# Inverse roots of queries, keys and attention results computed by GpSimd instead of VectorE

## The reference, cut to what matters

```python
h = rms_norm(x, ln_attn_g[i])
dq, dk, dv, mq, mk, mv = jnp.split(h @ w_in[i], cuts, axis=-1)   # six sections of 512 columns
dq = rms_norm(dq.reshape(B, S, 4, 2, 64), qk_norm_g[i, 0])       # likewise dk, mq, mk
y_diff = diff_attention(...)                                     # a = p0 - lam * p1, then
out = rms_norm(out, sub_g) * (1.0 - lam_init)                    # over 128 values of a head
x = x + jnp.concatenate([y_diff, y_moba], axis=-1) @ w_out[i]
x = x + conv_ffn(rms_norm(x, ln_ffn_g[i]), ...)
```

## Time and profile before

| | |
|---|---|
| median of three runs | 2059.21 us (2058.15 to 2059.31) |
| the profiled execution's own time | 2058.32 us |
| its span | 2056.1 us |
| mean granted TensorE clock | 0.997 of full |
| busy: PE, DVE, ACT, POOL | 2009.4, 1338.4, 957.1, 160.8 us |
| PE idle while the profile names a releaser or issue, longest group | 5.0 us in 6 times |
| layer 0 of the first block up to its feed forward | about the first 130 us |
| the same stage of layer 1 | about 350 to 465 us |

### The profile page before, as it was taken

One profiled execution on the slowest core, in us unless ns is written; L12 is line 12 of the kernel. 1 busy time (PEld: TensorE's weight loads), 2 busy tenths in 40 slices (PEclk: granted clock), 3 DMA queues, 4 the chain that ended last, 5 costly groups with the idle time before them and its releaser, 6 DMA issues.

```text
span 2056.1 us, 33524 instructions
## 1 busy us (share of the span) xinstructions
PE 2009.4 (98%) x13138; PEld 1738.2 (85%) x13138; DVE 1338.4 (65%) x2363; ACT 957.1 (47%) x1574; POOL 160.8 (8%) x169
## 2 busy tenths in 40 slices
PE   9999999999999999999999999999999999999998
PEld 7778998878999887878888788888878899888997
DVE  6767667767877348384445556868566595775675
ACT  4655555555555443353322453233246544455443
POOL 2001000000110100001200001111110000100110
PEclk9999999999999999999999999999999999999999
DMA  9447665535555422222222104534234244441654
GB/s 252 147 138 250 229 215 204 175 103 175 185 185 185 143 94 73 72 77 68 92 92 92 52 32 156 201 106 162 92 126 163 84 144 124 149 159 53 202 167 133
DMA packets 79707, 285.55 MB, mean 139 GB/s; under 512 B 8976, under 2 KB 9644, under 8 KB 79552
## 3 DMA queue, kind: packets, MB, share of 16 engines
q1 hardware_dynamic: 71136, 256.93, 37.6%
q10 hardware_dynamic: 6416, 19.51, 2.7%
q0 software_dynamic: 2000, 6.97, 1.3%
HBM read 277.55 MB, written 5.83 MB: 138 GB/s over the span
## 4 chain that ended last, share of the span: by engine, by line
PE 76%; DVE 13%; ACT 7%; issue 3%; DMA 1%; DVEq 0%; ACTq 0%; POOL 0%; SPq 0%
PE pb L1125 14%; PE pb L1127 14%; PE pb L1126 14%; PE pb L1138 6%; PE pb L1140 6%; PE pb L1139 6%; DVE SPL L2223 4%; ACT SPH L1638 3%; PE pb L1144 2%; PE pb L1303 2%; PE pb L1497 2%; PE pb L1304 2%; PE pb L1305 2%; PE pb L1478 2%; DVE GW L2556 1%
## 5 line engine op out<-in xcount | busy, mean ns | idle before, releaser
L2223 DVE TENSOR_TENSOR SPL<-RAW,SPH 128x1024 fp32r<-128x1024 f32 x460 | 559.4, 1232 | 387.0 <-ACT SPH L1638 366.1
L1638 ACT ACTIVATE SPH<-RAW 128x1024 fp32r<-128x1024 f32 x462 | 477.6, 1052 | 221.3 <-PE pb L1127 110.7
L1125 PE MATMUL pb<-HTH,SPH 128*128 128x256 f32 (+1 forms) x1304 | 445.7, 342 | 8.7 <-POOL HTL L2890 3.7
L1127 PE MATMUL pb<-HTH,SPL 128*128 128x256 f32 (+1 forms) x1304 | 436.6, 335 | 0.0
L1126 PE MATMUL pb<-HTL,SPH 128*128 128x256 f32 (+1 forms) x1304 | 436.2, 335 | 0.0
L1125 PEld LDWEIGHTS pb<-HTH,SPH 128*128 128x128 f32 x1304 | 246.6, 189 | 37.1 <-ACT HTH L1687 3.2
L1127 PEld LDWEIGHTS pb<-HTH,SPL 128*128 128x128 f32 x1304 | 246.7, 189 | 26.2
L1126 PEld LDWEIGHTS pb<-HTL,SPH 128*128 128x128 f32 x1304 | 246.5, 189 | 24.7
L1138 PE MATMUL pb<-SPH,HTH 128*128 128x512 f32 x640 | 254.4, 397 | 2.2 <-DVE SPL L2223 1.4
L1140 PE MATMUL pb<-SPL,HTH 128*128 128x512 f32 x640 | 249.9, 391 | 0.0
L1139 PE MATMUL pb<-SPH,HTL 128*128 128x512 f32 x640 | 249.7, 390 | 0.0
(11 more groups left out here) (298 smaller groups left out, 2869.4 us busy)
## 6 DMA issues: line engine op xcount, KB each, us to landing
RAW<-in_w_up SPq DMA_DIRECT2D x88, 512.0 KB, 4.6
RAW<-in_wa SPq DMA_DIRECT2D x64, 512.0 KB, 3.5
RAW<-in_w_in SPq DMA_DIRECT2D x48, 512.0 KB, 4.9
RAW<-in_wmg SPq DMA_DIRECT2D x48, 512.0 KB, 3.5
RAW<-in_wbr SPq DMA_DIRECT2D x48, 512.0 KB, 3.5
RAW<-in_w_down SPq DMA_DIRECT2D x44, 512.0 KB, 4.7
RAW<-in_w_ada SPq DMA_DIRECT2D x24, 512.0 KB, 4.8
ARAW<-in_w_ada ACTq DMA_DIRECT2D x24, 512.0 KB, 3.9
```

The costliest lines, as they stand in the source:

```text
L1125: T.matmul(o, wh[:, kt, :], xh[:, kt, n0:n1], start=kt == 0, stop=False)
L1127: m = T.matmul(o, wl[:, kt, :], xh[:, kt, n0:n1], start=False, stop=kt == 7)
L1638: A.activation(hi, raw, ACT.Copy, scale=1.0).then_inc(*act.tick(s["hi"], ("u", u)))
L2223: W.tensor_tensor(lo, raw, hi.bitcast(F32), SUB).then_inc(*dve.tick(s["lo_dve"], ("u", u)))
```

## The change

For layers 0 and 1 of the first block the roots are made on POOL. `qk_scale` gets a POOL part: two scalings with the mean's epsilon (16 values a partition in all), then one `pow` with a constant tile of -0.5. `y` gets a POOL part of four operations that depend on each other: multiply, scale and add, `pow`, multiply. They signal a new semaphore, `root_pool`. DVE keeps the sums and the multiplications into QKN and YN, and waits for `root_pool` where it computed roots before. The epsilon column SE loses its factors of c, since c belonged to the Newton steps. The new one-column tile HALF is filled at the start. POOL's `qk_scale` begins with waits on the memset of HALF, on `pool.last`, on DVE's sums and on SE.

```diff
--- before.py
+++ after.py
@@ -991,7 +991,7 @@
            "out_act",
            "lo_dve", "const_dve", "norm_dve", "qkv_dve", "soft_dve", "ffn_dve", "gla_dve", "branch_dve", "attn_dve",
            "out_dve",
-           "lo_pool", "norm_pool", "ffn_pool", "gla_pool", "branch_pool")
+           "lo_pool", "norm_pool", "ffn_pool", "gla_pool", "branch_pool", "root_pool")
 DMAS = ("raw0", "raw1", "raw2", "raw3", "raw4", "ada0", "ada1", "ada2", "x_in0", "x_in1", "par", "par2", "strips", "lamr", "const", "ctx", "bias",
         "table", "spill0", "spill1", "wdec", "x_back", "out")
 
@@ -2288,9 +2288,7 @@
         dve.wait_ge(n, ("sq", tag))
         rsqrt(n, ("rs", tag), sb["SS"][:, 4 + t0:6 + t0], sb["SS"][:, t0:t0 + 2], 1.0 / 1024, 2)
         if tag[0] == "a":
-            c = 0.375
-            W.tensor_scalar(sb["SE"][:, 0:2], sb["SS"][:, t0:t0 + 2], EPS / (1024 * c ** 2), (EPS / c) ** 2, MUL,
-                            ADD).then_inc(*dve.tick(n, ("se", tag)))
+            W.tensor_scalar(sb["SE"][:, 0:2], sb["SS"][:, t0:t0 + 2], EPS / 1024, EPS ** 2, MUL, ADD).then_inc(*dve.tick(n, ("se", tag)))
             return
         if tag[0] == "f":
             return
@@ -2345,12 +2343,8 @@
                             axis=AX.X, op=ADD, negate=None).then_inc(*dve.tick(q, ("qs", l, sec, t)))
 
     def qk_scale(l, sec):
-        q, QS = s["qkv_dve"], sb["QS"]
-        dve.wait_ge(q, ("qs", l, sec, 1))
-        dve.wait_ge(s["norm_dve"], ("se", f"a{l}"))
-        rsqrt(q, ("qr", l, sec), QS[:, 1, 0:16], QS[:, 0, 0:16], 1.0 / 64, 16,
-              [sb["SE"][:, t:t + 1] for t in range(2)])
-        dve.wait_ge(q, ("qr", l, sec))
+        QS = sb["QS"]
+        dve.wait_ge(s["root_pool"], ("qr", l, sec))
         for t in range(2):
             name = ("qkv", l, sec, t)
             if sec in (0, 1):
@@ -2416,16 +2410,7 @@
         dve.wait_ge(s["soft_act"], ("yq", l, g))
         W.tensor_reduce(out=sb["QSY"][:, 0, 0:4], in_=sb["SQY"][:, :].rearrange("p (g d) -> p g d", d=128), axis=AX.X,
                         op=ADD, negate=None).then_inc(*dve.tick(v, ("ys", l, g)))
-        dve.wait_ge(v, ("ys", l, g))
-        dve.wait_ge(v, ("r2", l, 4 * g + 3))
-        ss, rs = (sb["QSY"][:, i, 0:4].rearrange("p (i t) -> p i t", t=2) for i in range(2))
-        sums, squares = (V(R[:, i, 8 * g:8 * g + 1], [4, 2], [1, 2]) for i in (2, 3))
-        W.tensor_tensor(ss, ss, squares, MUL).then_inc(*dve.tick(v))
-        dve.wait_ge(*dve.last)
-        rsqrt(v, ("yr", l, g), sb["QSY"][:, 1, 0:4], sb["QSY"][:, 0, 0:4], 1.0 / 128, 4)
-        dve.wait_ge(v, ("yr", l, g))
-        W.tensor_tensor(rs, rs, sums, MUL).then_inc(*dve.tick(v))
-        dve.wait_ge(*dve.last)
+        dve.wait_ge(s["root_pool"], ("yr", l, g))
         W.tensor_tensor(yo, o, V(sb["QSY"][:, 1, 0:1], [2, per], [1, 2], [0, dv]), MUL).then_inc(
             *dve.free(*k.read(name)))
 
@@ -2830,6 +2815,7 @@
         for o, i in ((sb["OH"][0:32, 0:384], "onehot"), (sb["RB"][0:32, 0:12], "rel_bias"),
                      (sb["MROW"][0:12, 0:384], "maskrow")):
             G.dma_start(o, k.args[i]).then_inc(*pool.tick(s["strips"]))
+        G.memset(sb["HALF"][:, :], -0.5).then_inc(*pool.tick(s["root_pool"], "half"))
         G.memset(sb["QP1"][0:64, :, :], 0.0).then_inc(*pool.tick(s["gla_pool"]))
         pool.wait_ge(s["raw2"], ("u", 2))
         G.dma_start(sb["LAMR"][:, :], k.args["lamr"]).then_inc(*pool.tick(s["lamr"]))
@@ -2846,6 +2832,37 @@
         G.memset(sb["QP0"][64:128, base:base + 2, :], 0.0).then_inc(
             *pool.tick(s["gla_pool"], ("qp", l, sec, half)))
 
+    def qk_scale(l, sec):
+        QS, x = sb["QS"], sb["RS"][:, 0, 16:32]
+        pool.wait_ge(s["root_pool"], "half")
+        pool.wait_ge(*pool.last)
+        pool.wait_ge(s["qkv_dve"], ("qs", l, sec, 1))
+        pool.wait_ge(s["norm_dve"], ("se", f"a{l}"))
+        for t in range(2):
+            G.tensor_scalar(x[:, t * 8:t * 8 + 8], QS[:, 0, t * 8:t * 8 + 8], 1.0 / 64,
+                            sb["SE"][:, t:t + 1], MUL, ADD).then_inc(*pool.tick(s["root_pool"]))
+        pool.wait_ge(*pool.last)
+        G.tensor_tensor(QS[:, 1, 0:16], x, V(sb["HALF"][:, 0:1], [0, 16]), ALU.pow).then_inc(
+            *pool.tick(s["root_pool"], ("qr", l, sec)))
+
+    def y(l, g):
+        if g >= 2:
+            return
+        v, r, R = s["soft_dve"], s["root_pool"], sb["RR"]
+        ss, rs = (sb["QSY"][:, i, 0:4].rearrange("p (i t) -> p i t", t=2) for i in range(2))
+        sums, squares = (V(R[:, i, 8 * g:8 * g + 1], [4, 2], [1, 2]) for i in (2, 3))
+        x = sb["RS"][:, 1, 16:20].rearrange("p (i t) -> p i t", t=2)
+        pool.wait_ge(*pool.last)
+        pool.wait_ge(v, ("ys", l, g))
+        pool.wait_ge(v, ("r2", l, 4 * g + 3))
+        G.tensor_tensor(x, ss, squares, MUL).then_inc(*pool.tick(r))
+        pool.wait_ge(*pool.last)
+        G.tensor_scalar(x, x, 1.0 / 128, EPS, MUL, ADD).then_inc(*pool.tick(r))
+        pool.wait_ge(*pool.last)
+        G.tensor_tensor(x, x, V(sb["HALF"][:, 0:1], [0, 2], [0, 2]), ALU.pow).then_inc(*pool.tick(r))
+        pool.wait_ge(*pool.last)
+        G.tensor_tensor(rs, x, sums, MUL).then_inc(*pool.tick(r, ("yr", l, g)))
+
     def consts():
         k.past(pool, "ffn0")
         G.dma_start(sb["TRI"][:, :], k.args["tri"]).then_inc(*pool.tick(s["const"]))
@@ -2952,7 +2969,7 @@
         G.dma_start(sb["AFX"][:, 0:n, :], k.args["xscr"][0, 0:n * 128, :].rearrange("(t p) d -> p t d", p=128)
                     ).then_inc(*pool.tick(s["x_back"]))
 
-    does = {"start": start, "qk_turn": qk_turn, "split": split, "bias_rows": bias_rows, "consts": consts, "ctx_in": ctx_in,
+    does = {"start": start, "qk_turn": qk_turn, "qk_scale": qk_scale, "y": y, "split": split, "bias_rows": bias_rows, "consts": consts, "ctx_in": ctx_in,
             "bias_back": bias_back, "prod": prod, "up": up, "keep": keep, "gnorm": gnorm,
             "split_a": split_a, "split_z": split_z, "branch": branch, "x_back": x_back}
     for step, *a in sched.steps:
@@ -3128,6 +3145,7 @@
     p = m.put("CSP", p, [128, 8, 32])
     p = m.put("SEL", p, [128, 2, 2])
     p = m.put("SE", p, [128, 2])
+    p = m.put("HALF", p, [128, 1])
 
     m.put("FT", m.put("FC", qkt_at, [128, 2, 2, 256]), [128, 2, 256])
     p += (128 - base - p) % 512
```

## The result

The changed kernel takes 2080.08 us in the median (2079.95 to 2083.47, 4 runs) beside 2058.68 (2058.04 to 2059.31) before: 21.4 us slower, ratio 1.0111 (95% interval 1.0098 to 1.0123; the ratios given here and below are not the quotients of the two medians, which would be 1.0104 here). The forecast was slower with 2068, range 2062 to 2078. The direction and its main cause came out; the size did not, and the range was missed by 2.1 us. The profiled execution took 2083.47 us, its span 2081.7.

A forecast was written before the change was run, and what follows sets the result against it. PE, busy 98% of the span, bounds the kernel, so moved DVE work gains only where PE waits. 15.0 - 2.0 - 3.6 = +9.4 us on 2058.32 gave 2067.7, stated as 2068, range 2062 to 2078.

The forecast's parts named there:

- Where the first root waits: Layer 0, section 0: POOL's wait on its last noted operation, a DMA, holds it until the whole bias table has landed.
- L: Time when the bias table's last DMA lands and POOL can start the first root: 43.0 us, bounds 40.7 to 50.7.
- R: Time from DVE's sums to DVE's going on, for a root on POOL: 1.4 us, some 0.9 of it the power.
- section 4: Section 4 of each layer: DVE comes on 0.7 us earlier with the root on POOL, and PE gains that time.
- rival of a slow power: Each POOL power costs 2.69 us whatever its size, at first root, section 4 and `y`: +11.7, about 2080; chance 0.12.
- `y`: The two `y` of each layer: DVE 0.8 us earlier with POOL's root, and 0.3 at the second.
- unit 8 of layer 0: PE starts this w_in unit 13.9 us late behind the first root; with 1.1 for the clock, 15.0.
- section 1, layers 0 and 1: Roots there are off DVE's path, made by POOL while DVE splits, so they cost nothing: 0.
- the weights after the table, to unit 16: Layer 0: with the table landed first, weight loads come alone, as in layer 1, giving back 2.0 us.
- section 3: Roots there are hidden while DVE splits, but PE has no further wait to lose: 0.
- to the end of layer 1's attention: Sum of all terms over both layers the change touches: 15.0 - 2.0 - 3.6 = +9.4 us.
- the clock: PE's granted clock falls after its 12.5 us idle before the first turn: 1.1 us added, between 0.6 and 2.3.

The follow-up runs named there:

- Experiments 1, 2 and 3: Changed kernel without POOL's wait for the table's landing, 2069.21 us; kernel before with only that wait, on DVE, 2071.80; the first with table DMAs behind the first root, 2064.60.
- experiment 5: Changed kernel with added GpSimd powers of several sizes and one product beside layer 0's feed forward; 2078.35 us in a single execution.
- e12_warm18: Changed kernel with 18 useless matmuls in PSUM bank 7 ahead of PE's first turn of QKN; 2081.67 us, ratio 1.0111.
- experiment 2: Kernel before, all roots on DVE, with one added DVE wait for the bias table ahead of the first root; 2071.80 us, ratio 1.006.
- e3_dve00: Changed kernel with only the first root of layer 0 back on DVE; 2062.37 us, ratio 1.0013.
- e7_sec3: Kernel before with only the roots of section 3 of both layers on POOL; 2055.66 us, ratio 0.9991.
- e8_yonly: Kernel before with only the two y of each layer on POOL; 2057.56 us, ratio 0.9997.
- e1_nolast: Changed kernel with POOL's qk_scale waiting for its last compute operation, not the last operation noted; 2069.21 us, ratio 1.0045.
- e9_warm7: Changed kernel with 15 useless matmuls in PSUM bank 7 ahead of PE's first turn of QKN; 2081.04 us, ratio 1.0106.
- e2_order: Changed kernel with POOL waiting only for its last compute operation and the table's DMAs moved behind the first root; 2064.60 us, ratio 1.0021.

## Why the prediction was wrong

**Where the first root waits: right.** POOL stood at `pool.last` until the table had landed. L was put at 43.0; 44.64 less the later start of 1.28 is 43.4. Experiments 1, 2 and 3 show it from three sides: 10.4 us of POOL's time go with the wait, and the wait alone gives 14.9 us at unit 8.

**R, the step that failed.** "I take R = 1.4 ... some 0.9 for the power, between its ends and nearer to the lower, since 16 values a partition are nearer to 1 than to 1024." The power of 16 takes 2.93 us, above the upper end of 2.69, and R is 48.34 - 44.64 = 3.7. The bound was no bound: the dearest product says what 1024 products cost, not what a power costs, which goes by 0.158 us for each value (experiment 5). The range took even that bound, R = 3.2, for the first root only. R bears on section 1 and section 4 as well: +2.3, +2.7 and +3.8 us against the forecast in the table below, 8.8 together, where all of it missed by 8.5. The other errors nearly cancel. The forecast's rival of a slow power had the size nearly right (2.69, 2080) at a chance of 0.12. Its total was partly luck: it had a power cost 2.69 us whatever its size, which would make `y` dearer, where `y` gained a little, and it had nothing for section 1.

The terms, with the start of 1.28 us taken off:

| term | forecast | measured |
|---|---|---|
| unit 8 of layer 0 | +15.0 | +17.5 (L +0.4, R +2.3, the rest -0.2) |
| section 1, layers 0 and 1 | 0, "hidden" | +1.0 and +1.7 |
| the weights after the table, to unit 16 | -2.0 | -1.9, of which 0.8 to 1.7 is variation between traces |
| section 3 | 0 | -1.6 and -0.3 |
| section 4 | -0.7 and -0.7 | +1.2 and +1.2 |
| `y` | -1.1 and -1.1 | -0.4 and -0.4 |
| to the end of layer 1's attention | +9.4 | +17.9 |

**Sections 1, 3 and 4.** With R at 3.7 and more, section 1 is not hidden: DVE has one split (1.2 us) between sums and use, and on POOL the scalings take 1.46 us there against 0.65 elsewhere, with that split beside them. Section 3, with two waits of DVE between, hides all; there I had seen no wait of PE to lose, and overlooked those of 3.0 us in the earlier trace rows, one of which stood behind exactly that root. At section 4 and at the first root DVE waits for the whole of R.

**Unit 8.** I had it wait for its low part, 6.3 us behind the start of QKN. At full clock (e12_warm18) it starts 6.66 us behind, and the profile names ACT's copy of QP, which stands behind `lam` and two high parts in ACT's queue. In the changed kernel it waits for nothing: unit 7, stretched by the lower clock, ends later than that copy needs. So the forecast had 0.4 us too little for the wait and, with 1.1 for the clock instead of 0.65, about as much too much for the clock. The two errors cancel at unit 8, which is luck, and at unit 11 the clock costs nothing.

**The weights.** The reason that I gave for -2.0 does not hold as shown: the kernel of experiment 2 (15.1 to 13.1 in the table) would fit it, but e3_dve00, where the table lands as before, and e7_sec3 win as much at unit 16. Between 0.8 and 1.7 us of it is variation between traces.

**What stays open.** The landmarks give 17.9 us at the end of what the change touches, the medians 21.4. The start, 1.28 us later here, is between 0.31 us earlier and 1.34 later in the other traces, also where nothing ahead of it is changed, so no cause is shown for it. What comes behind the stages that the change touches can be read for the profiled executions, which are 25.1 us apart. In the changed kernel's, PE falls a further 1.4 us behind between 700 and 710 us and 2.1 us between 1560 and 1580, where the granted clock is at 1.2 GHz for a part (PEclk is the first of the last three numbers), while before it is 1.00 at the same steps (685 to 695 and 1540 to 1550 us there):

```profile
705.00:710.00 5.00, 4.25 (x21) 3.89 (x21) 1.51 (x2) 3.32 (x5) 1.39 (x2) 0.67 0.75 265
...
1560.00:1565.00 5.00, 4.33 (x19) 4.00 (x19) 4.63 (x12) 3.00 (x6) 1.21 (x2) 0.51 0.48 140
```

That is 3.5 of the 6 us that the landmarks leave open in that pair; some 2 us more gather over the last 400 us. Such stretches are not shown to come from the change: e8_yonly, no slower than before, falls 2 us behind at the same steps with the clock at 0.72 and 0.60 from 1535 to 1545 us. e12_warm18 has none at those first steps but one in layer 0's feed forward, at 0.77 from 205 to 210 us, and in that feed forward it loses 2.5 us (16.7 to 19.2 in the table), so its ratio is the same as the changed kernel's by another way. What share they have in the medians stays open.

The Trainium skill, GPSIMD Engine Reference, Instruction dispatch, has about 5.95 us for the first call of a freshly loaded kernel. The first power took 2.93 us and the later ones 2.90, and POOL had no gap before it but its waits, so this was no case of it. The same page, Specifications, says that GpSimd shares its SBUF interfaces with VectorE, with contention where a DVE instruction has two SBUF inputs; the splits are of that kind, and the rows of scalings and of a product beside them (1.46 against 0.65, 1.36 against 0.74) agree. The powers do not show it: 128x16 took 2.89 us with splits beside it and 2.90 to 2.93 without.

## What to carry to other kernels

Before work moves to another engine's queue, write down what stands ahead of it there, and what a wait "for my last operation" means if that operation is a DMA: here it turned an order between two instructions into a wait for 1.5 MB, and 16 of 21 us went with two edits of the order. A step that is hidden must be hidden by its full length in its new place: of eight roots only the two with more than 3.7 us between sums and use gained anything. An operation that no row shows has no upper bound from rows of other operations; put the range, and the chance of the dear case, accordingly.

## What the runs showed of the hardware

- A power on GpSimd costs 0.38 us and 0.158 us for each value a partition, and with half the partitions no less; a product of 16 values 0.22 us. DVE's whole chain of two scalings and eight dependent operations on the same 16 values takes 2.06 us.
- While VectorE ran splits (two inputs from SBUF), two scalings of 128x8 took 1.46 us instead of 0.65 and a product of 128x256 1.36 instead of 0.74. A power of 128x16 took 2.89 us beside splits, no more than without.
- PE's granted clock fell to 1.2 GHz when PE idled 4.1 us (e1_nolast) and 3.6 us (e9_warm7); with a wait of 1.1 us in e2_order and in e12_warm18 it stayed at 1.00. Eight transposes and most of a unit of 12 matmuls at 1.2 GHz cost 0.65 us at the next unit and nothing three units later, since PE had waits for other engines there.
- The landing of the same four DMAs varied: POOL went on 10.6 us behind the end of the last issue in the changed kernel's trace, 11.1 us in e12_warm18 and 12.5 us in e9_warm7.
